# Layer 0 attention written out by unit: V product one tile behind, squares of three units on GpSimd, no factors for a fifth unit

## The chip, the cores and the metric

The kernel runs on one core of one Trainium2 chip. The metric is device time in microseconds (us) of one execution, as the median of several runs. The engines are named as in the profile: PE is TensorE (its weight loads are listed apart as PEld), DVE is VectorE, ACT is ScalarE, POOL is GpSimd, and SP is the engine that here only issues DMAs.

## The reference, cut to what matters

A two-layer decoder trunk on one sequence of 1024 tokens with 1024 channels, in float32. Layer 0 mixes differential attention (4 heads, two softmax maps of 64 channels for each head, 128 value channels) with a pooling mixer, layer 1 a short convolution with dilated attention. Each layer ends in an output projection and a SwiGLU feed-forward block. The change touches layer 0 attention alone:

```python
def diff_attention(q, k, v, lam, slopes):
    def block(i):                       # 128 queries at a time
        s = einsum('bqmhd,bkmhd->bmhqk', qb, k) * scale
        s = s - slopes * dist           # ALiBi
        s = where(dist >= 0, s, -inf)   # causal
        p = softmax(s, axis=-1)
        a = p[:, 0] - lam * p[:, 1]
        return einsum('bhqk,bkhd->bqhd', a, v)
ya = rmsnorm(diff_attention(...), subln_gain) * (1.0 - lambda_init)   # per head, over its 128 channels
x = x + concatenate([ya, yb]) @ w_out
```

The RMS norm of each head is where the squares come from: every output row of 128 values is squared and summed.

## The kernel before

The program is one hand-written stream of instructions for each engine, tied together by counting semaphores. No scheduler orders anything: an engine runs its instructions in the order written, and each `wait_ge` in front of one holds back all that stands behind it on that engine.

Layer 0 attention runs over four **units** u, one for each head, and in each over eight **tiles** i of 128 queries. The causal rule makes tile i as wide as its 128(i+1) keys. The two softmax maps are m = 0 and m = 1. One step i does this:

- `score(m, i+2)` on PE (L682, L683) writes the scores of map m, two tiles ahead, into PSUM. It waits until DVE has read the tile before from the same PSUM place.
- `biased(m, i+1)` on DVE (L1610) adds bias and mask, writes to `PR[m][(i+1)%2]` and takes the row maximum. For map 0 it waits until `turn(i-1)` has read the buffer that it overwrites.
- `expo(m, i+1)` on ACT (L1157) takes the exponentials and their row sum.
- `combine(i)` on DVE (L1635, L1636, L1639) forms map 0 minus lambda times map 1, in place in `PR[0]`. L1639 has two inputs in SBUF.
- `turn(i)` on PE (L700) transposes the i+1 blocks of that tile into PSUM, `turned(i)` on ACT (L1005, to `PT`) copies them to SBUF, and `weigh(i)` on PE (L716) multiplies them by V.
- `scaled(i)` on ACT divides by the row sums. It reads the product twice: L1184 squares it into a junk tile `YJ` with the sum of squares in `YSS`, then L1005 writes `Y`.

PE's order in a step is score 0, turn(i), score 1, weigh(i). Only at i = 6 is turn(6) put ahead of score 0, because that score belongs to the next unit and waits for more.

The scores are made of split factors: each float32 operand is held as a high part in fp32r and the remainder. The high and low parts of a unit's K are stacked in `K1`, of its Q in `QST`, and `K2` is `K1` with its halves exchanged. For the **next** unit, ACT writes the high parts (`next_stack`: two of K at i = 1 and 2, four of Q at i = 6), POOL subtracts to get the low parts (L603), and as soon as the two K parts are complete, SP exchanges the halves with four DMAs (L470, L471). PE waits for these DMAs (`staged`) before tile 0 of the next unit, which is `score(0, 8)` of this unit, issued at i = 6. In unit 3 all of this is also done for a unit 4 that does not exist; two tiles of its scores are computed too.

POOL then adds epsilon to the unit's eight sums of squares (L609) and raises them to -0.5 (L611), and goes on to the K parts of the unit after. The pairs of units run in a loop of two passes over two written units.

Once attention is over, ACT copies four channels' blocks and the first output weights, DVE splits them, and PE goes on with the output projection.

## Time and profile before

| what | value |
| --- | --- |
| median of 3 runs | 2380.04 us (2377.31 to 2386.82) |
| the profiled execution, its own time | 2379.5 us |
| its span, first to last instruction | 2377.7 us |
| mean granted PE clock over the span | 0.982 |
| busy share of the span | PE 95%, DVE 55%, ACT 34%, POOL 20% |

The page cuts the span in 40 equal slices of 59 us. In almost all of them PE is busy nine tenths or more. Layer 0 attention is the dip in slices 4 to 6 (from about 224 to 355 us), where PE falls to seven tenths while DVE and ACT rise to eight tenths. Layer 1 attention is a like dip around 1500 us and is not touched. The times in the rows are us from the span's start.

### The profile page before, as it was taken

The numbers are of one execution on the slowest core, as the hardware profiler recorded it, in microseconds if no ns is written. First come the engines' busy times: TensorE is split into PE (matmuls) and PEld (weight loads), VectorE is DVE, ScalarE is ACT, GpSimd is POOL, SyncE is SP. The second block draws the span as 40 slices with busy tenths as digits, with TensorE's granted clock in tenths as the row PEclk, the third lists the DMA queues.
The fourth block names the chain that finished last, engine by engine and source line by source line (L and its number), as shares of the span: only waits on it lengthen the run. The fifth ranks groups of instructions, "written<-read, shape, count | busy, mean of one in ns | idle before, by whom it ended". The sixth has DMA issues, their size and how long they took to land.

```text
span 2377.7 us, 30768 instructions
## 1 busy us (share of the span) xinstructions
PE 2267.6 (95%) x10680; PEld 1878.8 (79%) x10680; DVE 1298.9 (55%) x1996; ACT 796.8 (34%) x1367; POOL 486.8 (20%) x358
## 2 busy tenths in 40 slices
PE   7999779999999999999999998989999999999998
PEld 6876667878888888887788877888878888888886
DVE  4335767755555555555412236666755555555554
ACT  4124882432222222222311126661532222222221
POOL 0022340332222222221200032220422222222220
PEclk9998999999999999999999998999999999999999
DMA  4021112011111111112111111111021111111112
GB/s 171 13 72 36 36 35 71 18 45 54 53 53 53 53 53 53 53 54 71 36 29 60 37 61 36 36 36 53 18 58 54 53 53 52 51 52 52 52 51 93
DMA packets 138271, 123.14 MB, mean 52 GB/s; under 512 B 6096, under 2 KB 113104, under 8 KB 138192
## 3 DMA queue, kind: packets, MB, share of 16 engines
q1 hardware_dynamic: 137904, 122.05, 16.9%
q8 instruction: 48, 0.79, 0.1%
q14 instruction: 31, 0.25, 0.0%
q10 hardware_dynamic: 288, 0.05, 0.0%
HBM read 107.40 MB, written 4.19 MB: 47 GB/s over the span
## 4 chain that ended last, share of the span: by engine, by line
PE 71%; issue 20%; ACT 4%; DVE 3%; POOL 2%; DMA 0%; DVEq 0%; POOLq 0%; ACTq 0%; SPq 0%
PE PS L964 11%; PE PS L965 11%; PE PS L966 11%; PE PS L630 9%; PE PS L632 9%; PE PS L631 9%; PE PS L716 4%; PE PS L700 2%; POOL QRS L593 1%; ACT PR L1157 1%; PE PS L682 1%; PE PS L683 1%; PE PS L648 1%; ACT PT L1005 1%; PE PS L919 0%
## 5 line engine op out<-in xcount | busy, mean ns | idle before, releaser
L1393 DVE TENSOR_TENSOR SLOTl<-SLOT,RING 128x512 fp32r<-128x512 f32 x294 | 203.4, 694 | 153.4 <-ACT RING L1005 153.4
L557 POOL TENSOR_TENSOR SLOT<-SLOT,SLOT 128x512 f32<-128x512 f32 x168 | 231.9, 1380 | 146.2 <-PE PS L966 103.0
L630 PE MATMUL PS<-WDh,HIDh 128*128 128x512 f32 x640 | 249.0, 389 | 0.0
L631 PE MATMUL PS<-WDl,HIDh 128*128 128x512 f32 x640 | 249.0, 389 | 0.0
L632 PE MATMUL PS<-WDh,HIDl 128*128 128x512 f32 x640 | 249.0, 389 | 0.0
L1819 DVE TENSOR_TENSOR X<-PS,X 128x512 f32<-128x512 f32 x320 | 212.1, 680 | 33.3 <-PE PS L632 33.2
L564 POOL TENSOR_TENSOR P<-U,P 128x512 f32<-128x512 f32 x42 | 54.3, 1293 | 802.6 <-DVE U L1788 802.6
L1005 ACT ACTIVATE RING<-SLOT 128x512 fp32r<-128x512 f32 x294 | 175.4, 623 | 105.3 <-POOL SLOT L557 67.5
L716 PE MATMUL PS<-V,PT 128*128 x864 | 117.7, 283 | 27.2 <-ACT PT L1005 23.5
L964 PE MATMUL PS<-B1h,RING 128*128 128x512 f32 x336 | 132.7, 395 | 8.8 <-DVE SLOTl L1393 8.8
L716 PEld LDWEIGHTS PS<-V,PT 128*128 128x128 f32 x864 | 107.3, 196 | 42.3 <-ACT PT L1005 28.1
L631 PEld LDWEIGHTS PS<-WDl,HIDh 128*128 128x128 f32 x640 | 120.1, 188 | 24.9
L630 PEld LDWEIGHTS PS<-WDh,HIDh 128*128 128x128 f32 x640 | 120.1, 188 | 24.9
L632 PEld LDWEIGHTS PS<-WDh,HIDl 128*128 128x128 f32 x640 | 120.1, 188 | 24.9
L1795 DVE TENSOR_TENSOR HID<-PS,U 128x512 f32<-128x512 f32 x42 | 29.1, 692 | 201.8 <-PE PS L966 201.8
L965 PE MATMUL PS<-B1l,RING 128*128 128x512 f32 x336 | 132.3, 394 | 0.0
L966 PE MATMUL PS<-B1h,SLOTl 128*128 128x512 f32 x336 | 132.3, 394 | 0.0
L593 POOL TENSOR_TENSOR QRS<-QMS,EXPO 128x8 f32<-128x8 f32 x32 | 52.0, 1637 | 390.4 <-DVE QMS L1544 390.2
L630 PE MATMUL PS<-WOh,HH 128*128 128x512 f32 x256 | 103.3, 404 | 10.8 <-DVE WOl L1393 10.0
L1610 DVE CUSTOM_DVE_ANT_0 PR<-PS,BIAS 128x128 f32<-128x128 f32 (+7 forms) x132 | 97.4, 740 | 29.7 <-PE PS L700 20.1
L1470 DVE TENSOR_TENSOR X<-PS,X 128x512 f32<-128x512 f32 x128 | 84.9, 686 | 49.0 <-PE PS L632 48.7
L1157 ACT ACTIVATE PR<-PR,NMX 128x128 f32<-128x128 f32 (+7 forms) x132 | 100.2, 760 | 14.6 <-DVE NMX L1610 13.9
(277 smaller groups left out, 5321.1 us busy)
## 6 DMA issues: line engine op xcount, KB each, us to landing
SLOT<-in_ffn_w_gate SPq DMA_DIRECT2D x84, 256.0 KB, 3.0
SLOT<-in_ffn_w_up SPq DMA_DIRECT2D x84, 256.0 KB, 2.8
WDs<-in_ffn_w_down SPq DMA_DIRECT2D x40, 512.0 KB, 3.5
K<-K SPq DMA_DIRECT2D x32, 256.0 KB, 4.4
RG<-in_od_w_in SPq DMA_DIRECT2D x12, 512.0 KB, 3.8
RQ<-in_ev_w_in SPq DMA_DIRECT2D x8, 512.0 KB, 3.8
RD<-in_ev_w_out SPq DMA_DIRECT2D x4, 1024.0 KB, 4.9
RQ<-in_od_w_in SPq DMA_DIRECT2D x8, 512.0 KB, 3.7
```

The source lines that it names most:

```text
L557: nc.gpsimd.tensor_tensor(at_w[dst], at_w[x], at_w[y], op).then_inc(w_sum, 1)
L630: pe.matmul(dst, lh, rh, start=first, stop=False)
L631: pe.matmul(dst, lh, rl, start=False, stop=False)
L632: return pe.matmul(dst, ll, rh, start=False, stop=last)
L716: last = pe.matmul(weighed(L, m, i), PT[m][:, P * j:P * j + P], V[:, j, bass.ds(off, w)], start=(j == 0), stop=(j == i))
L964: pe.matmul(dst, lh, rh[:, k, :], start=k == 0 and not adds_on, stop=False, skip_group_check=adds_on)
L965: pe.matmul(dst, lh, rl[:, k, :], start=False, stop=False, skip_group_check=adds_on)
L966: last = pe.matmul(dst, ll, rh[:, k, :], start=False, stop=k == 3, skip_group_check=adds_on)
L1005: return nc.scalar.activation(dst, src, ACT.Copy, **kw)
L1157: nc.scalar.activation(pr, pr, ACT.Exp, bias=NMX[:, c:c + 1], scale=-1.0, accum_out=DEN[:, c:c + 1]).then_inc(s_ex[m][L], 1)
L1393: return v.tensor_tensor(dst, src, hi.bitcast(F32), ALU.subtract)
L1819: v.tensor_tensor(xs, bank(4 + t % 4), xs, ALU.add).then_inc(fd_add[L], 1)
```

## The change

The two-pass loop of layer 0 becomes four units written out, with constant semaphore counts and addresses. Within that:

- **PE.** The order of a step becomes score 0, weigh(i-1), turn(i), score 1. The special order at i = 6 is gone, and its waits on `staged` and the low parts now stand in front of score 0, weigh(5) and turn(6). `PT` has two buffers (the second was idle in this layer), `RDN` four columns of pairs.
- **ACT.** `scaled` runs two tiles behind. The squares (L1184) are kept for unit 3 alone. The last step of unit 3 has no exponentials for a next unit.
- **POOL.** For units 0, 1 and 2 the squares come here, as eight instructions for each half unit: one product of 128x512, six additions that fold 128 columns to 2, and one that gives the sum. They stand behind the low parts of the next unit and ahead of the low parts of the unit after.
- **Fifth unit.** No high or low parts, no DMAs, no bias table and no scores for it.
- Layer 1 keeps its loop; its counts are adapted.

```diff
+                def squares(u, half):
+                    n = 8 * (2 * u + half)
+                    pool.wait_ge(o_ok[0][0], 2 + NT * u + 4 * half + 4)
+                    ys = Y[:, 4 * half:4 * half + 4, P * u:P * u + P]
+                    nc.gpsimd.tensor_tensor(YQ[:], ys, ys, ALU.mult).then_inc(y_fold, 1)
+                    for k, w in enumerate((64, 32, 16, 8, 4, 2)):
+                        pool.wait_ge(y_fold, n + k + 1)
+                        nc.gpsimd.tensor_tensor(YQ[:, :, 0:w], YQ[:, :, 0:w], YQ[:, :, w:2 * w], ALU.add).then_inc(y_fold, 1)
+                    ...
+                if L == 0:
+                    pool.wait_ge(mx_pe, 4)
+                    for u in range(UNITS):
+                        if u + 1 < UNITS:
+                            for k in range(STACKS):
+                                low_stack(k, (u + 1) % 2, u + 1, stacks_before(0, u + 1) + k)
+                            pool.wait_ge(stack_lo, stacks_before(0, u + 2))
+                            squares(u, 0)
+                            squares(u, 1)
+                        else:
+                            pool.wait_ge(y_sq, NT)
...
-                            if L == 0:
-                                if i == NT - 2:
-                                    turn(L, 0, g, h, i)
-                                    pe.wait_ge(staged[1 - b], 64 * (3 * L + it + 2) if b else 64 * (2 * L + it + 1))
-                                    pe.wait_ge(stack_lo, following + 3)
-                                    score(L, 0, b, g, i + 2)
-                                    pe.wait_ge(stack_lo, following + 4)
-                                else:
-                                    score(L, 0, b, g, i + 2)
-                                    turn(L, 0, g, h, i)
-                                score(L, 1, b, g, i + 2)
-                                weigh(L, 0, u, g, h, i)
+                            if i == NT - 2 and more:
+                                pe.wait_ge(staged[1 - b], 64 * (u // 2 + b + 1))
+                                pe.wait_ge(stack_lo, following + 3)
+                            if more:
+                                score(0, 0, b, g, i + 2)
+
+                            if i > 0:
+                                weigh(0, 0, u, g, 0, i - 1)
+                            elif u > 0:
+                                weigh(0, 0, u - 1, g - NT, 0, NT - 1)
+                            turn(0, 0, g, 0, i)
+                            if i == NT - 2 and more:
+                                pe.wait_ge(stack_lo, following + 4)
+                            if more:
+                                score(0, 1, b, g, i + 2)
...
+                            if i == NT - 2 and not last:
+                                next_stack(g, 1 - b, u + 1, 2, 3)
+                            if i < NT - 1 or not last:
+                                expo(0, g, i + 1)
+                            if g + i >= 2:
+                                scaled(g + i - 2)
+                            if i < NT - 1 or not last:
+                                expo(1, g, i + 1)
+                            turned(0, g, i)
+                            if i in (1, 2) and not last:
+                                next_stack(g, 1 - b, u + 1, i - 1)
+                            if i == NT - 2 and not last:
+                                next_stack(g, 1 - b, u + 1, 4, 5)
```

PE at i = 6 of unit 0, before. `K_166` and `QST_75` are the next unit's factors; the rows with IDN and PR are turn, those with V and PT weigh.

```order
L700 MATMUL PS<-IDN,PR_176 128x128 [waits c_ok]
L700 MATMUL PS<-IDN,PR_176 128x128 x6
L823 ISA
L824 REGISTER_ALU [waits staged1]
L676 REGISTER_ALU [waits stack_lo]
L682 MATMUL PS<-K_166,QST_75 128x128 [waits s_mxA0]
L683 MATMUL PS<-K_170,QST_75 128x128
L826 REGISTER_ALU
L682 MATMUL PS<-K_167,QST_76 128x128 [waits s_mxB0,stack_lo]
```

The same place now:

```order
L708 MATMUL PS<-K_166,QST_75 128x128 [waits s_mxA0,stack_lo,staged1]
L709 MATMUL PS<-K_170,QST_75 128x128
L744 MATMUL PS<-V,PT_175 128x128 [waits o_okA0,t_eaA0]
L744 MATMUL PS<-V,PT_175 128x128 x5
L728 MATMUL PS<-IDN,PR_176 128x128 [waits c_ok,t_eaA0]
L728 MATMUL PS<-IDN,PR_176 128x128 x6
L708 MATMUL PS<-K_167,QST_76 128x128 [waits s_mxB0,stack_lo]
L709 MATMUL PS<-K_171,QST_76 128x128
```

The wait for the DMAs (staged1) moved from behind turn(6) to ahead of it, and weigh(5) stands between the two.

POOL between the last low part of a unit and the first of the unit after, before:

```order
L603 TENSOR_TENSOR QST_76<-QK,QST_76 64x768
L607 ISA
L609 ISA [waits stack_lo,y_sq]
L609 TENSOR_TENSOR YSS<-YSS,EPSP 128x8
L611 REGISTER_ALU [waits y_ms]
L611 TENSOR_TENSOR YRS<-YSS,EXPO 128x8
L601 ISA [waits y_rs]
L602 REGISTER_ALU [waits stack_hi]
L603 TENSOR_TENSOR K_164<-QK,K_164 64x1024 [waits stack_lo]
```

And now; the eight rows from `YQ<-Y` to `YSS<-YQ` stand there twice, the second half unit's are left out here:

```order
L602 TENSOR_TENSOR QST_76<-QK,QST_76 64x768 [waits stack_lo,stack_hi]
L609 TENSOR_TENSOR YQ<-Y 128x512 [waits o_okA0,stack_lo]
L612 TENSOR_TENSOR YQ<-YQ 128x4x64 [waits y_fold]
L612 TENSOR_TENSOR YQ<-YQ 128x4x32 [waits y_fold]
L612 TENSOR_TENSOR YQ<-YQ 128x4x16 [waits y_fold]
L612 TENSOR_TENSOR YQ<-YQ 128x4x8 [waits y_fold]
L612 TENSOR_TENSOR YQ<-YQ 128x4x4 [waits y_fold]
L612 TENSOR_TENSOR YQ<-YQ 128x4x2 [waits y_fold]
L615 TENSOR_TENSOR YSS<-YQ 128x4 [waits y_fold]
...
L630 TENSOR_TENSOR YSS<-YSS,EPSP 128x8 [waits y_fold]
L632 TENSOR_TENSOR YRS<-YSS,EXPO 128x8 [waits y_ms]
L602 TENSOR_TENSOR K_166<-QK,K_166 64x1024 [waits stack_lo,stack_hi,y_rs]
```

Sixteen instructions, each waiting for the one before, came between the low parts of one unit and the K parts of the unit after.

## Rows read from the trace of the kernel before

**Rows 1.** Windows: us, PE, PEld, DVE, ACT, POOL busy; clock, DMA share, GB/s.

```profile
224.00:370.00 146.00, 110.39 (x658) 91.03 (x659) 104.00 (x248) 114.21 (x289) 50.42 (x32) 0.92 0.14 37
```

**Rows 2.** Waits from 224 to 375 us: us in total, times, longest.

```profile
PE PS L716 <- ACT PT L1005: 23.5, 29, 1.6
...
DVE PR L1610 <- PE PS L700: 20.1, 15, 3.5
```

**Rows 3.** Timeline of PE, unit 1, i = 3 to 6: start, us, form.

```profile
271.04 0.60 PE L700 MATMUL PS<-IDN,PR 128*128 128x128 f32 x4
...
275.30 0.71 PE L700 MATMUL PS<-IDN,PR 128*128 128x128 f32 x5
...
277.06 1.38 PE L716 MATMUL PS<-V,PT 128*128 x10 [0.22 <-ACT PT L1005]
278.19 0.48 PE L682 MATMUL PS<-K,QST 128*128 128x512 f32 x1
...
279.20 0.82 PE L700 MATMUL PS<-IDN,PR 128*128 128x128 f32 x6
...
281.66 1.60 PE L716 MATMUL PS<-V,PT 128*128 x12 [0.68 <-ACT PT L1005]
...
283.80 0.30 PE L682 MATMUL PS<-K,QST 128*128 128x128 f32 x1
```

**Rows 4.** Timeline of DVE, units 1 and 2.

```profile
276.20 1.09 DVE L1610 CUSTOM_DVE_ANT_0 PR<-PS,BIAS 128x896 f32<-128x896 f32 x1 [0.88 <-PE PS L700]
...
277.72 1.02 DVE L1639 SCALAR_TENSOR_TENSOR PR<-PR,SCB,PR 128x768 f32<-128x768 f32 x1
...
293.65 1.28 DVE L1579 SCALAR_TENSOR_TENSOR BIAS<-DIST,SM,MASK 128x1024 f32<-128x1024 f32 x1
```

**Rows 5.** Timeline of ACT, unit 1.

```profile
278.56 0.37 ACT L1184 ACTIVATE YJ<-PS,RDN 128x128 f32<-128x128 f32 x1
...
285.33 0.90 ACT L1005 ACTIVATE PT<-PS 128x896 f32<-128x896 f32 x1
```

**Rows 6.** Timeline of POOL, end of unit 1 and start of unit 2.

```profile
287.04 3.90 POOL L603 TENSOR_TENSOR QST<-QK,QST 64x768 fp32r<-64x768 f32 x2 [2.56 <-ACT QST L1005]
293.15 0.20 POOL L609 TENSOR_TENSOR YSS<-YSS,EPSP 128x8 f32 x1 [2.21 <-ACT YJ L1184]
293.53 1.64 POOL L611 TENSOR_TENSOR YRS<-YSS,EXPO 128x8 f32 x1 [0.17 <-POOL YSS L609]
298.54 2.37 POOL L603 TENSOR_TENSOR K<-QK,K 64x1024 fp32r<-64x1024 f32 x1 [3.38 <-ACT K L1005]
301.92 2.37 POOL L603 TENSOR_TENSOR K<-QK,K 64x1024 fp32r<-64x1024 f32 x1 [1.00 <-ACT K L1005]
```

**Rows 7.** The last of four exchange DMAs of unit 2, and landing of L471.

```profile
306.11 1.12 SPq L471 DMA_DIRECT2D K<-K  x1
...
DMA to landing us min/median/max: 2.3/3.8/5.6
```

**Rows 8.** Timelines of POOL and DVE where both read SBUF.

```profile
458.38 1.29 POOL L541 TENSOR_TENSOR F0T3s<-F0T2s,F0T3s 128x512 f32<-128x512 f32 x1
...
248.71 0.72 POOL L603 TENSOR_TENSOR QST<-QK,QST 64x256 fp32r<-64x256 f32 x1 [8.66 <-ACT QST L1005]
249.67 1.30 POOL L603 TENSOR_TENSOR QST<-QK,QST 64x256 fp32r<-64x256 f32 x1 [0.23 <-POOL QST L603]
...
248.88 1.49 DVE L1639 SCALAR_TENSOR_TENSOR PR<-PR,SCB,PR 128x896 f32<-128x896 f32 x1
```

**Rows 9.** Timeline of PE: score(0, 8) of units 0 and 2.

```profile
251.17 0.31 PE L682 MATMUL PS<-K,QST 128*128 128x128 f32 x1
...
314.94 0.30 PE L682 MATMUL PS<-K,QST 128*128 128x128 f32 x1
```

**Rows 10.** Windows, columns as in rows 1: PE nearly idle, then its clock.

```profile
252.00:254.00 2.00, 0.42 (x4) 0.35 (x4) 1.16 (x5) 2.00 (x4) 0.00 (x0) 1.00 0.00 0
...
256.00:258.00 2.00, 2.00 (x12) 2.00 (x11) 0.00 (x0) 1.10 (x5) 1.76 (x2) 0.51 0.00 0
```

More of the change, by code:

```diff
@@ L808, in _ @@
                         score(L, m, 0, 0, i)
-                with pe.Fori(0, 2) as it:
-                    for b in range(2):
-                        u = 2 * it + b
-                        g, h = 16 * it + 8 * b, 8 * it + 4 * b
-                        following = stacks_before(L, u + 1)
+                if L == 0:
+                    for u in range(UNITS):
+                        b, g = u % 2, NT * u
+                        following = stacks_before(0, u + 1)
                         for i in range(NT):
+                            more = u + 1 < UNITS or i < NT - 2
@@ new lines, in _ @@
+                            turn(0, 0, g, 0, i)
[3 more added lines that the diff above has]
+                                score(0, 1, b, g, i + 2)
+                    weigh(0, 0, UNITS - 1, NT * (UNITS - 1), 0, NT - 1)
+                else:
+                    with pe.Fori(0, 2) as it:
+                        for b in range(2):
+                            u = 2 * it + b
+                            g, h = 16 * it + 8 * b, 8 * it + 4 * b
+                            following = stacks_before(L, u + 1)
+                            for i in range(NT):
+                                if i == 0:
+                                    pe.wait_ge(stack_lo, following)
+                                if i == 2 and b == 0:
+                                    pe.wait_ge(staged_rest, 64 * L + 64)
@@ new lines, in scaled @@
+                def scaled(n):
+                    u, i = n // NT, n % NT
+                    c = 2 * (i % 4)
+                    act.wait_ge(o_pe[0][0], n + 1)
+                    if u == UNITS - 1:
+                        act.wait_ge(o_ok[0][0], n + 2)
+                        nc.scalar.activation(YJ[:], weighed(0, 0, i), ACT.Square, scale=RDN[:, c:c + 1],
+                                             accum_out=YSS[:, n:n + 1]).then_inc(y_sq, 1)
+                    copy(Y[:, i, P * u:P * u + P], weighed(0, 0, i), scale=RDN[:, c:c + 1]).then_inc(o_ok[0][0], 1)
@@ new lines, in _, with turned, scaled, next_bias @@
+                if L == 0:
+                    for u in range(UNITS):
+                        b, g, last = u % 2, NT * u, u + 1 == UNITS
+                        for i in range(NT):
+                            if i < NT - 1 or not last:
+                                biased(0, b, g, i + 1)
+                            if i == 1 and not last:
+                                dve.wait_ge(s_mx[1][0], g + 1)
+                                bias(0, 1 - b, u + 1)
+                            combine(g, i)
+                            if i < NT - 1 or not last:
+                                biased(1, b, g, i + 1)
+                else:
+                    with dve.Fori(0, 2) as it:
+                        att.reg = per_iter * it
+                        for b in range(2):
+                            u = 2 * it + b
+                            g = 16 * it + 8 * b
+                            def turned(m, i):
+                                if i >= 4:
+                                    dve.wait_ge(t_pe[m][L], g + i + 3)
+                                    w = P * (i + 1)
+                                    v.tensor_copy(PT[m][:, HALF:w], turn_bank(1, m, i, 1)[:, 0:w - HALF]).then_inc(t_ed[m][1], 1)
+                            def scaled(m, i):
+                                c = m + 2 * (i % 2)
+                                dve.wait_ge(s_ex[m][1], g + i + 1)
+                                att.link(v.reciprocal(RDN[:, c:c + 1], DEN[:, c:c + 1]))
+                                dve.wait_ge(o_pe[m][1], g + i + 1)
+                                v.tensor_scalar(Y[:, i, bass.ds(u * P + HD * m, HD)], weighed(1, m, i), RDN[:, c:c + 1], None,
+                                                ALU.mult).then_inc(o_ok[m][1], 1)
+                            def next_bias(m):
+                                dve.wait_ge(s_mx[m][1], g + 9)
+                                bias(m, 1 - b, 2 * u + 2 + m)
+                            for i in range(NT):
```

227 lines of the change are left out of this document (99 added, 128 removed).

## The prediction

> **What bounds the kernel now.** First the windows over the attention stage of layer 0 [rows 1]: of 146 us ACT is busy 114, PE 110, DVE 104, POOL 50. No engine is full, so the stage runs at the pace of a chain that crosses engines, and the question for each edit is whether it stands on that chain. Next the list of waits [rows 2]: PE waits 23.5 us in 29 places for ACT's copy of the transposed tile, and DVE 20.1 us for the transposes. So the chain is turn, copy, product with V, next score, next turn. The timeline of PE shows one round of it [rows 3]: turn(4) starts at 275.30, weigh(4) at 277.06 behind the copy, score(0, 7) at 278.19, turn(5) at 279.20. That is 3.90 us a step, and PE is in order, so the product and the score both stand between two turns.
>
> **V product one tile behind.** The step becomes score 0, weigh(i-1), turn(i). This looks as if it took the product out of the chain, but the score put ahead of it has a wait of its own. score(0, 7) needs biased(0, 6), and biased(0, 6) overwrites the buffer that turn(4) reads. It starts at 276.20, 0.19 after turn(4) ends [rows 3, 4]. The new round from turn(4) to turn(5) is therefore turn 0.71, handover 0.19, biased 1.09, handover 0.06, score 1.01 (278.19 to 279.20), weigh 1.13 (277.06 to 278.19): 4.19 us, 0.3 more than now [rows 3, 4]. One tile earlier each piece is smaller (0.11, 0.13, 0.12 and 0.23), 3.6 in all, against 4.26 measured from 271.04 to 275.30: 0.6 less [rows 3]. The product's cost grows fastest with i, so the order gains at small i. I take two steps at 0.6, one small one at 0.1, minus 0.3: **1.0 us a unit**, between 0 and 2. In units 1 and 2 it counts only if nothing later holds the unit back, and something does.
>
> **Squares off ACT.** 24 squares leave ACT, 0.36 us each from start to start (278.56 to 278.92), 8.6 us in all [rows 5]. The rounds above do not pass through them. They are slack on ACT, and I count nothing for them in units 0 to 2; the bound from the other side is a rival below.
>
> **Squares on POOL.** For each half unit, the 128x512 product costs 1.29 [rows 8]. 64x256 takes 0.72 and 64x768 half of 3.90 less a gap, 1.83, so 0.54 us for each 256 columns above a fixed 0.18 [rows 6, 8]. The folds have 256, 128, 64, 32, 16, 8 and 4 elements: 0.72, 0.45, 0.31, 0.25, 0.21, 0.20 and 0.19. With the product that is 3.6 us. Each waits for the one before; that gap is 0.17 between the two statistics instructions and 0.23 between two low parts [rows 6, 8]. Eight gaps make 1.4 to 1.9. A half is 5.0 to 5.5, I take 5.1, **10.2 us a unit**. POOL was two thirds idle, so by busy time this is free. By place it is not: it stands ahead of the K parts that the next score(0, 8) waits for.
>
> **The chain that this makes**, from one score(0, 8) to the next:
> - On PE score 0.3, weigh(5) 1.4, turn(6) 0.95, then a handover 0.1 to ACT: 2.8. The shift of the wait ahead of turn(6) puts this piece on the chain.
> - From ACT's copy of tile 6 to the end of the last low part: 285.33 to 290.94, 5.6 [rows 5, 6].
> - Squares 10.2.
> - Epsilon and power, from 293.15 to 295.17 and a handover: 2.2 [rows 6].
> - Two K parts: 2.37 each and a gap, 4.9 [rows 6].
> - The DMAs: the K parts end at 304.29, the last of four is issued at 306.11 and lands 3.8 later (median): 5.6 [rows 6, 7].
>
> The sum is 31.3 us. It can't run undisturbed. DVE's two-input instructions and POOL shut each other out: L1639 with 896 columns took 1.49 at 248.88 while POOL worked from 248.71 to 249.43, and the POOL instruction behind took 1.30 instead of 0.72 [rows 8]. In the 17 us of squares, power and K parts, DVE has six combines of 128 to 768 columns. The widest takes 1.02 and each narrower one 0.13 less (1.28 at 1024 columns), 4.2 in all, and the bias table 1.28 [rows 4]. Seven gaps of 0.2 take up 1.4, which leaves 4.1. The Trainium skill, SBUF — State Buffer, section "Who interferes with whom", says that whichever starts first holds the shared ports for its whole instruction. By that rule the whole of each counts, as I do; if the two ran side by side, the forecast would be 8.2 us lower. **35.4 us a unit.**
>
> Measured now from score(0, 8) of unit 0 to that of unit 2: 63.8 us for two units [rows 9]. Two rounds of 35.4 are 70.8: **plus 7.0**. PE would run out of work at i = 6 of units 1 and 2 for some 5 us each.
>
> **The clock.** When PE was busy 0.42 of 2 us, its granted clock was 0.51 two windows later, which is the 1.2 GHz level [rows 10]. After a stall, the 2.7 us of PE work at the head of the chain would take twice as long. This counts once inside the two rounds and may count again after unit 2: **plus 2.7**, between 0 and 5.4.
>
> **What is gained at the ends.** Before score(0, 8) of unit 0: 1.0. After that of unit 2: unit 3 gains 1.0 by the order, 1.1 by the bias table of a fifth unit (1.28 on DVE right ahead of combine(1), [rows 4]), 0.6 because tiles 6 and 7 are no longer mixed with factors on ACT, and 0.7 in the last two steps of unit 2. Sum 3.4. The squares stay there, and so does the tail (last turn, copy, product, scaling). The earlier place of score(0, 8) inside step 6 shifts both ends by the same amount and cancels. **Minus 4.4**, between 2 and 7. Constant counts instead of registers I count at nothing: the waits in question are attributed to other engines [rows 2, 4].
>
> **Sum.** 7.0 + 2.7 - 4.4 = +5.3 us on the profiled execution's own 2379.5 us: **2384.8 us**. That execution lies 0.5 under the median of 2380.04, so against the median the change is +0.2%. About 0.5%, 12 us, is what a measurement of this kernel can tell from no change.
>
> **Rivals.**
> 1. *The POOL chain is short enough.* Gaps of 0.17, the locked ports cost little, the clock stays: 31.3 x 2 - 63.8 = -1.2, minus 4.4: 2373.9. For it: POOL often fits between two combines today. Against it: with POOL never idle, each combine must meet it. Chance 0.17.
> 2. *ACT sets the pace.* It is the busiest engine [rows 1]. Then 8.6 us of squares and the fifth unit's six high parts go (0.9 and 1.7 at tiles 6 and 7, two K parts of 1.0, as the factors of other units cost), some 13 us: 2366. For it: the profile's chain names ACT often. Against it: it needs POOL's round under 28 us, less than its own rows sum to. Chance 0.13.
> 3. *Slower: the small folds are dear.* There are 16 short instructions in a round, 32 in two. The median run leaves the 0.5% band when the two rounds cost 6.6 more, that is from 0.21 us more for each. At 0.3 more it is +9.6: 2394.4. For it: the power of eight elements takes 1.64 [rows 6], so a short instruction is not always a cheap one, and a form of four rows of 2 to 64 columns is nowhere in the trace. Against it: the addition of 128x8 takes 0.20 [rows 6]. A second fall of the clock adds to it. Chance 0.20.
> 4. My forecast, a round of 34 to 37 us: 0.50, all of it within 12 us of now.
>
> **Range and chances.** The low end takes in rival 1 and a bit of rival 2's gain, the high end rival 3 with 0.3 us: 2371 to 2396. Faster by over 0.5%: 0.13. Within: 0.66. Slower: 0.21.
>
> **What would show it.** In the profile after: in units 1 and 2 PE idles several us ahead of the first score of the next unit, released by the DMA K<-K; from one such score to the next 34 to 37 us, where it was 31.1 and 32.6; POOL busy without a break from the last low part to the second K part, at 10 to 11 us for the squares; in unit 0 no such wait, and turn(4) to turn(5) about 4.2. Unit 3 two to three us shorter than before; the granted clock at 0.5 behind the stalls. Wrong if the first score of the next unit never waits for a DMA (then rival 2 or a round shorter than I think), or if YQ instructions of few elements take 0.4 and more (rival 3).

## The result and the profile after

The changed kernel takes 2388.52 us (median of 20 runs, 2381.31 to 2393.81), the kernel before on the same chip 2379.55 (median of 20, 2376.99 to 2386.82). The ratio is 1.0034, with an interval of 1.0025 to 1.0043. That is inside the 0.5% that the prediction took as the limit of no change, but it is a real loss: 8 us by the ratio, 9 by the medians. The profiled execution took 2390.1 us with a span of 2388.1, which is 10.4 us more than the span before.

Where do these 10.4 us come in? Both profiles start layer 0 attention, turn(0) of unit 0, at 227.33 us, so marks can be compared directly:

| mark | before | after | difference |
| --- | --- | --- | --- |
| turn(6) of unit 0 | 250.43 | 251.25 | +0.8 |
| turn(6) of unit 2 | 314.24 | 320.13 | +5.9 |
| turn(6) of unit 3 | 345.23 | 348.98 | +3.8 |
| first product of the output projection | 361.66 | 367.66 | +6.0 |
| first power of the norm behind it | 422.78 | 427.63 | +4.9 |
| first `biased` of layer 1 attention | 1440.99 | 1447.38 | +6.4 |
| last `biased` of layer 1 attention | 1587.74 | 1600.24 | +12.5 |
| end | 2377.7 | 2388.1 | +10.4 |

So 6 us come from the attention stage that was changed, and as much again from layer 1 attention, whose text is the same; 2 us come back behind it. These are single executions, and the marks move between executions of one text. But two of the runs below have the same instructions in this stage, the one that moves layer 1's loop (as changed) and the one that adds transposes alone (as before), and they give nearly the same difference: from turn(0) of unit 0 to the first output product 137.9 and 131.5 us, 6.3 apart, where here it is 140.3 and 134.3.

The first group of windows (us, busy us of PE, PEld, DVE, ACT, POOL; granted clock, DMA share, GB/s) shows the stage that [rows 1] showed of before:

```profile
224.00:370.00 146.00, 110.38 (x630) 91.65 (x631) 102.07 (x236) 101.83 (x231) 64.14 (x74) 0.87 0.10 25
```

ACT has lost 12 us of work and POOL has gained 14, as planned, but PE's granted clock has gone from 0.92 to 0.87. The list of waits from 224 to 375 us, against [rows 2]:

```profile
PE PS L708 <- POOL QST L602: 10.1, 6, 1.8
ACT PT L1047 <- PE PS L728: 10.0, 7, 3.3
```

The 23.5 us of PE behind ACT's copies are nearly gone (5.3 are left); that is the V product moved one tile back. A wait that was short before has come in: PE's score for the low part of Q that POOL writes. PE's timeline has it twice in a unit, at i = 6 (128 columns) and at i = 0 (384 columns):

```profile
249.62 0.30 PE L708 MATMUL PS<-K,QST 128*128 128x128 f32 x1 [1.59 <-POOL QST L602]
...
284.06 0.30 PE L708 MATMUL PS<-K,QST 128*128 128x128 f32 x1 [1.56 <-POOL QST L602]
...
285.70 0.93 PE L728 MATMUL PS<-IDN,PR 128*128 128x128 f32 x7
...
292.88 0.44 PE L708 MATMUL PS<-K,QST 128*128 128x384 f32 x1 [1.76 <-POOL QST L602]
...
318.49 0.30 PE L708 MATMUL PS<-K,QST 128*128 128x128 f32 x1 [1.58 <-POOL QST L602]
```

These are the rows that answer to [rows 9]. From 249.62 to 284.06 and from there to 318.49 it is 34.4 us each. Behind the first wait of a unit stand weigh(5) and turn(6), behind the second weigh(7) and turn(0). Not all of them could have run in the gap. At i = 6 ACT's copy for weigh(5) ends at 282.86 and DVE's combine for turn(6) only at 284.90, after the wait is over:

```profile
282.07 0.79 ACT L1047 ACTIVATE PT<-PS 128x768 f32<-128x768 f32 x1
283.40 1.50 DVE L1686 SCALAR_TENSOR_TENSOR PR<-PR,SCB,PR 128x896 f32<-128x896 f32 x1
```

At i = 0 the copy for weigh(7) ends at 291.94, 0.9 before the score.

POOL's timeline of the same unit, against [rows 6]:

```profile
254.49 3.91 POOL L602 TENSOR_TENSOR QST<-QK,QST 64x768 fp32r<-64x768 f32 x2 [3.44 <-ACT QST L1047]
258.48 1.04 POOL L609 TENSOR_TENSOR YQ<-Y 128x512 f32<-128x512 f32 x1
259.60 3.43 POOL L612 TENSOR_TENSOR YQ<-YQ 128x256 f32<-128x256 f32 x6
263.11 0.20 POOL L615 TENSOR_TENSOR YSS<-YQ 128x4 f32<-128x4 f32 x1
263.38 1.04 POOL L609 TENSOR_TENSOR YQ<-Y 128x512 f32<-128x512 f32 x1
264.50 3.00 POOL L612 TENSOR_TENSOR YQ<-YQ 128x256 f32<-128x256 f32 x6
267.57 0.20 POOL L615 TENSOR_TENSOR YSS<-YQ 128x4 f32<-128x4 f32 x1
267.85 0.20 POOL L630 TENSOR_TENSOR YSS<-YSS,EPSP 128x8 f32<-128x8 f32 x1
268.14 1.64 POOL L632 TENSOR_TENSOR YRS<-YSS,EXPO 128x8 f32<-128x8 f32 x1
269.86 5.14 POOL L602 TENSOR_TENSOR K<-QK,K 64x1024 fp32r<-64x1024 f32 x2
283.24 2.25 POOL L602 TENSOR_TENSOR QST<-QK,QST 64x256 fp32r<-64x256 f32 x2 [8.24 <-ACT QST L1047]
```

The squares take 9.3 us a unit (258.48 to 267.77), and the K parts are done at 275.0. Then POOL is idle for 8.24 us. The last exchange DMA is issued behind them (SP's queue, against [rows 7]):

```profile
277.10 0.78 SPq L473 DMA_DIRECT2D K<-K  x1
```

Its issue ends at 277.88. With the median landing time of [rows 7], 3.8, that makes 281.7, and with the longest of this line in the stage, 5.1, 283.0. The score goes at 284.06, so the K chain is not what ends last. DVE, on the other side of the shared port, against [rows 4]:

```profile
263.38 1.32 DVE L1686 SCALAR_TENSOR_TENSOR PR<-PR,SCB,PR 128x256 f32<-128x256 f32 x1
...
266.81 0.62 DVE L1686 SCALAR_TENSOR_TENSOR PR<-PR,SCB,PR 128x384 f32<-128x384 f32 x1
...
271.03 1.74 DVE L1686 SCALAR_TENSOR_TENSOR PR<-PR,SCB,PR 128x512 f32<-128x512 f32 x1
```

The combine of 256 columns takes twice as long as that of 384. And PE's clock in these windows:

```profile
262.00:264.00 2.00, 0.71 (x4) 0.44 (x3) 1.93 (x4) 0.71 (x3) 1.84 (x3) 1.00 0.00 0
264.00:266.00 2.00, 1.15 (x4) 0.79 (x4) 1.49 (x4) 0.79 (x3) 1.76 (x4) 0.69 0.00 0
266.00:268.00 2.00, 2.00 (x7) 1.36 (x6) 1.93 (x7) 2.00 (x5) 1.61 (x6) 0.50 0.00 0
268.00:270.00 2.00, 2.00 (x9) 1.90 (x10) 0.27 (x3) 1.26 (x4) 1.84 (x3) 0.50 0.00 0
```

PE was busy 0.71 and 1.15 of 2 us there, and then it runs at 0.50, the 1.2 GHz level. The same fall comes again at 298 to 305 us. The kernel before has no fall in the middle of unit 1 or 2; its fall of [rows 10] lies ahead of turn(0) of unit 1.

The tail of unit 3, on PE. Before, turn(7) took 1.03 and weigh(7) 2.05:

```profile
348.98 0.95 PE L728 MATMUL PS<-IDN,PR 128*128 128x128 f32 x7 [0.16 <-DVE PR L1686]
352.10 2.10 PE L744 MATMUL PS<-V,PT 128*128 128x128 f32 x14 [2.17 <-ACT PT L1047]
354.00 1.92 PE L728 MATMUL PS<-IDN,PR 128*128 128x128 f32 x8
357.02 3.62 PE L744 MATMUL PS<-V,PT 128*128 128x128 f32 x16 [1.11 <-ACT PT L1047]
```

Last, DVE in layer 1 attention, at the first `biased` of the second pass of the loop, before and after:

```profile
1518.60 0.42 DVE L1610 CUSTOM_DVE_ANT_0 PR<-PS,BIAS 128x256 f32<-128x256 f32 x1 [0.40 <-issue]
```

```profile
1529.24 0.42 DVE L1668 CUSTOM_DVE_ANT_0 PR<-PS,BIAS 128x256 f32<-128x256 f32 x1 [3.13 <-issue]
```

DVE stands for 3.13 us although nothing in the profile holds it back, and PE waits 4.00 us for it where it waited 1.27.

### The profile page after: what moved, and what is told of

Its sections match the earlier page's. It is cut to its first block, busy times and chain, and to the rows that moved or that the text cites. A ratio compares the mean times of both kernels' runs of the same rounds, so it can differ in the third digit from the quotient of the medians.

```text
span 2388.1 us, 30402 instructions
## 1 busy us (share of the span) xinstructions
PE 2276.0 (95%) x10672; PEld 1886.9 (79%) x10672; DVE 1301.8 (55%) x1991; ACT 784.9 (33%) x1309; POOL 500.5 (21%) x400
## 3 DMA queue, kind: packets, MB, share of 16 engines
HBM read 107.40 MB, written 4.19 MB: 47 GB/s over the span
## 4 chain that ended last, share of the span: by engine, by line
PE 67%; issue 14%; DVE 2%; POOL 1%; ACT 1%; DVEq 0%; POOLq 0%; ACTq 0%
PE PS L1006 11%; PE PS L1007 11%; PE PS L1008 11%; PE PS L656 9%; PE PS L658 9%; PE PS L657 9%; PE PS L744 2%; PE PS L728 1%; POOL QRS L595 1%; PE PS L708 1%; PE PS L674 1%; PE PS L709 0%; PE PS L961 0%; PE PS L960 0%; PE PS L959 0%
## 5 line engine op out<-in xcount | busy, mean ns | idle before, releaser
L1880 DVE TENSOR_TENSOR X<-PS,X 128x512 f32<-128x512 f32 x320 | 212.5, 681 | 33.3 <-PE PS L658 33.2
L744 PE MATMUL PS<-V,PT 128*128 (+1 forms) x864 | 118.3, 284 | 7.5 <-ACT PT L1047 5.3
L708 PE MATMUL PS<-K,QST 128*128 128x512 f32 (+2 forms) x196 | 85.6, 437 | 32.6 <-DVE NMX L1668 15.5
```

The source lines that it names most:

```text
L708: pe.matmul(dst, q, K1[b][m][:, c0:c1], start=True, stop=False)
L744: last = pe.matmul(weighed(L, m, i), PT[m if L else i % 2][:, P * j:P * j + P], V[:, j, bass.ds(off, w)], start=(j == 0), stop=(j == i))
L1880: v.tensor_tensor(xs, bank(4 + t % 4), xs, ALU.add).then_inc(fd_add[L], 1)
```

## The experiments

The experiments ran on three occasions, four kernels each. Absolute times are compared only within one; over all of them the ratio to the kernel before counts, and the lengths inside the profiles. "A unit" is the distance of two turn(6) from each other, unit 0 to 1 and unit 1 to 2. It is 34.5 and 34.4 us in the changed kernel, and 32.7 and 31.1 before. The 32.7 holds the fall of the clock of [rows 10]: in the run with the transposes alone, which has the same instructions there and no fall, it is 31.0 and 31.1.

### Squares back on ACT

```diff
-                            squares(u, 0)
-                            squares(u, 1)
-                        else:
-                            pool.wait_ge(y_sq, NT)
+                        pool.wait_ge(y_sq, NT * u + NT)
...
-                    if u == UNITS - 1:
+                    if True:
                         act.wait_ge(o_ok[0][0], n + 2)
```

> The changed kernel with the squares of all four units back on ScalarE (all else as changed). Marks are the first score of the next unit, score(0, 8), in units 0, 1 and 2, and the first product of the output projection; in the changed kernel 249.6, 284.1, 318.5 and 367.7 us, so 34.4 us from mark to mark. Theory A (the squares on GpSimd keep VectorE's combine off the shared ports in steps 0 to 2 of each unit, 1.0 + 1.3 + 1.1 us): 31.0 us from mark to mark, and combines of 0.35, 0.48 and 0.75 us again, for 1.1, 1.3 and 1.7. Theory B (ScalarE was the relief that mattered, 0.36 us for each square): the gain by the ports is eaten by 8 x 0.36 us on ScalarE, and it stays at 33 to 34.5 us. Theory C, my prediction (a chain through GpSimd and the DMAs): also about 31, with the DMAs no longer last. The whole: A -6 to -7 us against the changed kernel, so about +2 us against the kernel before; B no change.

Measured: 2385.66 us, ratio 1.0022 (1.0012 to 1.0031). A unit takes 32.1 and 32.4. So the squares on POOL cost 2.2 us a unit in this order of PE. The combine of 256 columns is back at its own length:

```profile
261.16 0.48 DVE L1685 SCALAR_TENSOR_TENSOR PR<-PR,SCB,PR 128x256 f32<-128x256 f32 x1
...
267.01 0.75 DVE L1685 SCALAR_TENSOR_TENSOR PR<-PR,SCB,PR 128x512 f32<-128x512 f32 x1
```

1.32 - 0.48 and 1.74 - 0.75 make 1.8 us a unit that DVE lost to POOL. The kernel is still slower than before, so the squares are not the whole of it.

### No squares at all in units 0 to 2

```diff
-                            squares(u, 0)
-                            squares(u, 1)
+                            pool.wait_ge(o_ok[0][0], 2 + NT * u + NT)
```

> The changed kernel without any squares in units 0 to 2, on no engine (their sums of squares are a constant 1.0). Theory A: 31.0 us from mark to mark, the same as with squares on ScalarE, since ScalarE has slack. Theory B: clearly less than with the squares on ScalarE, by up to 2.9 us a unit.

Measured, one execution: 2384.66 us; a unit takes 32.1 and 32.3, the same as with the squares on ACT. ACT has room for them: they cost nothing there, so taking them away could gain nothing. That settles rival 2.

### PE's two waits behind the work that doesn't need them

```diff
+                            if early:                      # i in (0, NT - 2)
+                                behind()                   # weigh of the tile before
+                            if i == NT - 2 and early:
+                                turn(0, 0, g, 0, i)
                             if i == 0:
                                 pe.wait_ge(stack_lo, following)
                             if i == NT - 2 and more:
                                 pe.wait_ge(staged[1 - b], 64 * (u // 2 + b + 1))
                                 pe.wait_ge(stack_lo, following + 3)
                             if more:
                                 score(0, 0, b, g, i + 2)
...
```

In the other steps weigh and turn stay behind the score.

> The changed kernel, but in step 6 TensorE does the V product and the transposes of tile 6 ahead of the wait for the next unit's factors, and in step 0 the V product of the last tile ahead of the wait for the last low parts. Squares stay on GpSimd. Theory A: the two waits of 1.6 and 1.8 us in front of the scores cost nothing any more, 2.2 us less from mark to mark counted at tile 6's transposes (32.2 instead of 34.4). Theory C: the chain from mark to mark loses TensorE's piece of 2.8 us, so 31.6 or whatever else binds. Rival: they cost nothing as it is, because VectorE's combines set the pace there: 34.4.

> The changed kernel with PE's two waits behind the work that doesn't need them, squares on POOL as in the changed kernel: the same text as the run with one look, now timed against the kernel before. If the two waits are what the new order costs: 2375 again, 4 us under the kernel before, ratio about 0.998. If that look was luck of one execution: 2380 or more.

Measured: one execution gave 2375.35 us. Timed on the next occasion, the same text took 2379.06 (ten runs, 2377.77 to 2382.54), ratio 1.0001 (0.9992 to 1.0011). The first was a good execution, not a typical one: in its profile the granted clock fell less often in layer 1 attention. What holds in both profiles is the unit, 31.5 us in the first and 31.5 and 31.3 in the second. So with both waits moved a unit is 3.0 us shorter, and with the squares on POOL and this order the loss against before is gone.

The 1.6 and 1.8 us of the waits sum to 3.4, which looks like the same amount, but they are not what comes back. From turn(5) to turn(7) it is 9.1 us with the wait at i = 6 in front and 9.1 with it behind. From turn(7) to turn(0), where the other wait stands, 5.27 become 4.39. The rest, 2.1 us, comes from the steps between turn(0) and turn(4). DVE's combines meet POOL there still:

```profile
262.42 1.13 DVE L1694 SCALAR_TENSOR_TENSOR PR<-PR,SCB,PR 128x384 f32<-128x384 f32 x1
...
269.08 1.96 DVE L1694 SCALAR_TENSOR_TENSOR PR<-PR,SCB,PR 128x640 f32<-128x640 f32 x1
```

Without POOL they take 0.62 and 0.89, so DVE loses 1.6 us a unit, nearly as much as in the changed kernel. What is mostly missing is the fall of the clock. With PE's new order and the wait at i = 0 in front, units 1 and 2 had one in their first steps 9 times out of 10, over five profiles; with both waits behind, 2 times out of 12, over six. But the fall alone isn't the price either: the unit of 31.3 us has one.

### The order of the kernel before, with the rest of the change

Squares on ACT, four units written out, no factors for a fifth unit, but weigh(i) in its own step and turn(6) ahead of the waits:

```diff
+                            if i == NT - 2:
+                                turn(0, 0, g, 0, i)
...
                             if more:
                                 score(0, 1, b, g, i + 2)
-                    weigh(0, 0, UNITS - 1, NT * (UNITS - 1), 0, NT - 1)
+                            weigh(0, 0, u, g, 0, i)
```

> TensorE's order of the kernel before (the V product in its own tile's step, tile 6 transposed ahead of the waits), squares of all units on ScalarE, written out by unit and without the factors, table and scores of a fifth unit. What is left of the change is then the written-out form, ScalarE's scaling two tiles behind, two buffers for the transposed tile, and no fifth unit. Theory A: 31.1 us from unit to unit as before, unit 3 shorter by 1 to 2 us, but its tail, where TensorE now has little to do, may fall to the lower clock level as in the changed kernel (last transposes 1.92 us instead of 1.03) and cost 2 us: first product of the output projection at 360 to 362 us (before 361.7). The whole: -2 to +1 us against the kernel before. Rival (the order with the product one tile behind is itself a gain, 0.6 us in two steps of each unit): this one is slower than the run with squares on ScalarE.

Measured: 2381.69 us, ratio 1.0008 (0.9998 to 1.0018). A unit takes 31.0 and 31.0, and the first output product comes 130.2 us after turn(0) of unit 0, where it was 134.3 before. The attention stage is thus 4.1 us shorter in the profile and the kernel no faster. Most of the 4.1 is the execution that it is compared with: the run with the transposes alone has the old stage with fewer falls of the clock and takes 131.5, so the stage gains about 1.3. Layer 1 takes that away: DVE stands 2.95 us at the loop's second pass here too, as in every kernel of this study in which DVE's layer 0 is written out and nothing else moves the loop.

### Both: squares on ACT and the waits behind

> The changed kernel with both edits at once: the squares of all units on ACT, and PE's two waits for the next unit's factors behind the work that doesn't need them (weigh(7) at i = 0; weigh(5) and turn(6) at i = 6). Theory A (squares on POOL lengthen DVE's combines through the shared port, and with the waits in front this is passed on; with the waits behind, part of it is absorbed): a unit 30.9 to 31.3 us against 31.5 with the squares on POOL, the first output product 1 to 2 us earlier than there, time 2373 to 2375. Theory D (with the waits behind, the place of the squares no longer matters): 31.5 a unit, 2375. Theory B (ACT is relieved by the change and needs it): a unit 32 or more, 2378 or more.

> The text with squares on ACT and both waits behind, timed a second time. It took 2384.4, though in its profile the attention stage is 0.5 us shorter than with the squares on POOL, which took 2379.1; and the same text with the transposes of the identity took 2376.0. If 2384.4 holds: something outside layer 0 attention differs between two texts that differ in 24 instructions. If it comes out at 2378 to 2380: an earlier level of this text on that occasion, and differences of some 4 us between runs of one occasion are then no evidence.

Measured: 2384.36, ratio 1.0025 (1.0015 to 1.0034), and on the next occasion 2382.33, ratio 1.0010 (1.0001 to 1.0019). Inside the first of the two profiles a unit takes 30.9 and 30.9, the shortest of all. Theory A's numbers for the unit hold: with the waits behind, the squares on POOL cost 0.5 us a unit, no longer 2.2. And the product with V one tile behind is worth nothing: 30.9 here, 31.0 in its own step.

Step by step, from turn(6) of unit 1 to turn(6) of unit 2:

| step, us | before | changed | squares on ACT | waits behind | both |
| --- | --- | --- | --- | --- | --- |
| turn(6) to turn(7) | 5.08 | 4.15 | 4.15 | 4.79 | 4.79 |
| turn(7) to turn(0) | 4.39 | 5.27 | 5.28 | 4.39 | 4.59 |
| turn(0) to turn(4) | 13.86 | 15.87 | 13.84 | 13.76 | 13.01 |
| turn(4) to turn(5) | 3.90 | 4.19 | 4.20 | 4.22 | 4.22 |
| turn(5) to turn(6) | 3.90 | 4.95 | 4.95 | 4.31 | 4.32 |

Either edit alone takes 2 us out of turn(0) to turn(4), and both together 2.9, so the 2.2 and the 3.0 don't add up. How large the loss there is depends on which combines meet POOL and on whether the clock is down at the time; the runs don't split it further.

But the whole time fits none of the theories. It lies 2 to 6 us above the text with the squares on POOL, though its units are shorter, and where those microseconds lie differs from one execution to the next: in the profile of the second occasion the clock fell twice more, at the start of unit 1 and behind its turn(6). Why this text should draw more such falls than its neighbour is open.

### Filling PE's idle stretches at the end of the stage

```diff
+                            if u == UNITS - 1 and i >= NT - 2:
+                                pe.wait_ge(s_mx[0][0], g + 9)
+                                warm(12 if i == NT - 2 else 6)
                     weigh(0, 0, UNITS - 1, NT * (UNITS - 1), 0, NT - 1)
+                    warm(32)
```

> As the run with squares on ACT and waits behind, plus transposes of the identity on PE into a PSUM place that nobody reads: 12 after turn(6) of unit 3, 6 after turn(7), 32 after weigh(7), at 0.13 us each by turn(7). They do no work; they fill PE's idle stretches at the end of the stage. Theory T (the tail of unit 3 and the start of the output projection are slow because PE ran idle there and its granted clock fell to 0.50; the two tiles of scores of the fifth unit had filled that gap before): turn(7) takes 1.03 and weigh(7) 2.05 again, the tail from turn(6) to the first output product 16.5 us instead of 18.7, and the products after it run at a granted clock near 1.00, another 2 us: 3 to 4 us less than the run without them. Against it: if the clock falls all the same, or the tail waits for ACT and DVE, the time is the same within 1 us, or more by the transposes themselves.

Measured: 2375.97 us, ratio 0.9989 (0.9979 to 0.9999), 8.4 us under the same text without them on the same chip. PE's timeline of the tail:

```profile
341.85 1.83 PE L745 MATMUL PS<-V,PT 128*128 128x128 f32 x14 [0.86 <-ACT PT L1060]
...
345.66 2.05 PE L745 MATMUL PS<-V,PT 128*128 128x128 f32 x16 [0.46 <-ACT PT L1060]
347.55 3.66 PE L711 MATMUL PS<-IDN 128*128 128x128 f32 x32
354.74 0.47 PE L653 MATMUL PS<-WOh,HH 128*128 128x512 f32 x1 [3.54 <-DVE WOl L1466]
355.05 0.40 PE L654 MATMUL PS<-WOl,HH 128*128 128x512 f32 x1
...
356.29 0.63 PE L655 MATMUL PS<-WOh,HL 128*128 128x512 f32 x1
```

The same text without them had a fall of the clock in weigh(6):

```profile
344.05 3.36 PE L741 MATMUL PS<-V,PT 128*128 128x128 f32 x14 [2.17 <-ACT PT L1052]
```

With them weigh(6) takes 1.83, turn(7) 1.04 instead of 1.17, and turn(6) to the first output product 16.0 us (338.72 to 354.74) instead of 17.6; the 18.7 of the changed kernel is the longest of all. After the 32 transposes PE idles 3.54 us, and the clock still falls a few products later (0.63 for a product instead of 0.40). The tail and the products behind it, up to the first power of the norm, explain 2.8 of the 8.4 us. In the two profiles layer 1 attention differs by another 6.0 (156.26 and 150.25), with more falls of the clock in the longer one; why, stays open.

The idle 2.17 us are there in all ten profiles without a fifth unit and without transposes. The clock fell behind them in nine. In one, the first with the waits behind, it didn't, and its tail takes 16.0 us without any filling. So the fall is likely there, not certain.

### Layer 1's loop at another place in the program

```diff
                         split_qk(L, r)
+                        if L == 1 and r in (2, 3):
+                            for _ in range(96):
+                                dve.sem_inc(waited, 1)
```

> The changed kernel with 192 semaphore increments more on DVE, 96 each behind two splits of layer 1's weights where DVE waits 10 to 15 us anyway. They move all later DVE instructions by 192 places. Theory F (the 3.13 us that DVE stands without a releaser between the two passes of layer 1's attention loop, 0.40 in the kernel before, is the fetch of instructions behind a taken branch, and depends on where in the program the loop lies): the 3.13 changes, to about 0.4 if the new place is a good one, and PE's wait there from 4.0 to 1.3. Theory G (it comes from the data or the queues of the new layer 0): it stays at 3.1. Place a little further or nearer may be needed: one look can show F but not exclude it.

Measured, one execution: 2384.64 us. DVE at the second pass of the loop, and PE's score that waits for it:

```profile
1521.87 0.42 DVE L1671 CUSTOM_DVE_ANT_0 PR<-PS,BIAS 128x256 f32<-128x256 f32 x1 [0.42 <-issue]
```

```profile
1522.36 0.44 PE L708 MATMUL PS<-K,QST 128*128 128x384 f32 x1 [1.29 <-DVE NMX L1671]
```

The 3.13 us have become 0.42 and PE's wait is 1.29 again, with nothing changed but the number of instructions ahead of the loop. So the stall belongs to the place of the loop in DVE's program, and not to the new layer 0. The Trainium skill, Runtime: NRT & Kernel Launch, section "Instruction fetch mechanics", says that an engine prefetches instructions in order, in two blocks, and that a taken branch to a target outside them waits for a fetch; this fits what the runs show, and the runs add the price, 2.7 us. Distance from the first to the last `biased` of layer 1 attention: 146.75 us before, 152.86 after, 148.76 here.

### All of it

The two waits behind, squares on ACT, the transposes (54 instead of 32 at the end), the 192 increments:

> The changed kernel with everything that the runs so far point to: squares on ACT, PE's two waits behind, the transposes of the identity at the end of the stage (54 instead of 32 after weigh(7), so that they reach up to the first output product), and the 192 semaphore increments on DVE that move layer 1's loop. If the three effects are separate and add up: 2376.0 (the run without the last two edits) minus 2.7 for the loop of layer 1 minus about 0.8 for the first twelve output products at 0.40 us apart from 0.63: 2372 to 2373.5, ratio 0.9975. If layer 1's stall is made up by what follows it, as a rival says: 2375 to 2376.

Measured: 2372.95 us (6 runs), against 2380.22 of before on the same chip; ratio 0.9964 (0.9951 to 0.9976). This beats both kernels, that of before by 7 us in the medians and 8.6 by the ratio. The sum came out as expected, but not each term on its own, against the profile with 32 transposes: layer 1 attention is 1.5 us shorter (148.80 against 150.25 us) and not 2.7, since the clock fell at 1476 to 1482 us where it hadn't there; the stretch ahead of it is 1.2 us longer; and the output projection gains 1.6 us instead of 0.8. A unit takes 30.9, turn(6) of unit 3 to the first output product 16.1, and the products there start at full clock:

```profile
349.90 6.06 PE L711 MATMUL PS<-IDN 128*128 128x128 f32 x54
357.13 0.47 PE L653 MATMUL PS<-WOh,HH 128*128 128x512 f32 x1 [1.17 <-DVE WOl L1466]
357.43 0.39 PE L654 MATMUL PS<-WOl,HH 128*128 128x512 f32 x1
357.66 0.40 PE L655 MATMUL PS<-WOh,HL 128*128 128x512 f32 x1
357.89 0.40 PE L653 MATMUL PS<-WOh,HH 128*128 128x512 f32 x1
```

### The transposes alone, in the kernel before

```diff
+                if L == 0:
+                    pe.wait_ge(s_mx[0][0], 8 * UNITS + 2)
+                    for _ in range(54):
+                        pe.transpose(PS[:, 0:P], IDN[:], IDN[:])
```

> The kernel before, with 54 transposes of the identity on PE after the last weigh(7) of layer 0 and nothing else. Theory T (the clock at the start of the output projection costs time in both kernels): the first 12 output products 0.23 us apart instead of 0.43, 2.4 us in all, so 2376.5, ratio 0.999. If what follows is set by DVE's splits and not by PE: no change.

Measured: 2376.75 us, ratio 0.9987 (0.9978 to 0.9996), as theory T has it. In its profile the output projection up to the first power of the norm takes 58.6 us, where it was 61.1. About a third of what the best version gains can be had without the change.

### Only the wait at i = 6 behind

> The changed kernel with only one of PE's two waits moved: at i = 6 weigh(5) and turn(6) stand ahead of the waits and of the first score of the next unit; at i = 0 the wait for the four low parts of Q stays ahead of weigh(7) and turn(0). Squares on POOL. With both moved a unit took 31.5 us, with none 34.4. If each wait is paid for by its own length (1.6 at i = 6, 1.8 at i = 0): 33.0 to 33.3 a unit. If the wait at i = 0 alone spoils it: 34 or more. If it is only the one at i = 6: 31.5.

Measured, one execution: 2387.5 us, and the two units differ: 33.7 and 31.2. They are the same instructions. In the first, the clock fell at 264 to 270 us and one combine met POOL for long; in the second it didn't:

```profile
272.40 2.81 DVE L1694 SCALAR_TENSOR_TENSOR PR<-PR,SCB,PR 128x640 f32<-128x640 f32 x1
...
305.30 0.98 DVE L1694 SCALAR_TENSOR_TENSOR PR<-PR,SCB,PR 128x640 f32<-128x640 f32 x1
```

The second unit is as short as with both waits moved, though the wait at i = 0 stands ahead of weigh(7) and turn(7) to turn(0) takes 5.29 us: turn(0) to turn(4) takes only 12.65 there, and 15.07 in the first. So none of the three expectations fits both units. The waits have no fixed price; a fall of the clock, and the collisions that shift with it, make 2.4 us in one unit, more than either wait's own cost.

## Why the prediction was right, and where it was not

The forecast was 2384.8 us, 0.2% more, from a sum of +5.3 us; measured is +0.34%, 8 to 9 us. The range holds it and the side is right. But the steps did not all do what they were said to do, and errors cancelled: that the sum came near was luck. Every term of the sum lies ahead of the first output product, where the two profiles differ by +6.0; the rest of the 8 to 9 us was in no term. Measured from turn(6) to turn(6):

| piece | forecast | measured |
| --- | --- | --- |
| up to turn(6) of unit 0 | -1.0 | +0.8 |
| units 1 and 2, clock included | +9.7 | +5.1 |
| from there to the first output product | -3.4 | +0.1 |
| layer 1 attention | 0 | +6.1, of it 2.7 by the loop's place |

- **V product one tile behind.** The hand-worked rounds were right to the tenth: turn(4) to turn(5) is 4.19 in unit 3 of the changed kernel (340.85 to 345.04), and turn(3) to turn(4) 3.61. But the 1.0 us a unit is not there: 30.9 with the new order, 31.0 with the old one, squares on ACT in both. Between these two, turn(2) to turn(4) gains 0.7 (7.17 against 7.90), where the sum had 1.3 for three steps, and not only turn(4) to turn(5) loses 0.4 but turn(5) to turn(6) too. The sum charged one late step and left out the second.
- **Squares off ACT.** Nothing, as said; the run without any squares shows it.
- **Squares on POOL.** 9.3 us instead of 10.2. The product of an operand with itself takes 1.04, where the bound row with two operands had 1.29 [rows 8]; the folds of 64 elements and fewer cost 0.20 to 0.33 each where nothing meets them (0.56 and 1.06 for the one of 8 elements when it met DVE), so rival 3 falls.
- **POOL's chain to the K DMAs.** This is the step that failed. Its undisturbed sum was good: up to the landing of the last DMA the round takes 34.4 less 2.4, 32.0, against 31.3. But the 4.1 us for the shared port were put on POOL, which lost 0.7 (1.6 if the squares' shorter length is counted). It was DVE that lost, 1.8 a unit, on the chain of combine and turn. The rule of the Trainium skill (SBUF — State Buffer, "Who interferes with whom") is that the engine that issues first holds the shared ports and the other waits. DVE's 1.74 for 512 columns and 1.32 for 256 agree with it, and so does the other way round: POOL's fold of 8 elements took 1.06 instead of 0.20 when DVE's bias table had started 0.34 ahead of it. Which engine is the later one must come from rows, and here it was mostly DVE.
- **What PE waits for.** The prediction named the DMA K<-K as the releaser of the first score of the next unit, and it never is. By the prediction's own sign ("Wrong if the first score of the next unit never waits for a DMA") the mechanism was wrong, and the round of 34.4 inside its 34 to 37 was luck. It is the low part of Q, a few steps away: last score of the unit, ACT's high part, POOL's low part. That chain stood in the kernel before as well (POOL's low parts at 281.99 and 287.04, the second in [rows 6]), but there turn(6) and the products with V lay ahead of the waits, and PE waited 0.3 us for them in unit 1. The prediction put turn(6) and weigh(5) behind the wait on POOL's chain and missed the second wait, at i = 0, that now holds back weigh(7). Against the 31.1 of before a unit is 3.3 us longer: 0.9 at i = 0, 2.0 between turn(0) and turn(4), 0.3 at turn(4) to turn(5) by the order, and 0.1 around i = 6, where the prediction had some 5 us.
- **The clock.** Forecast 2.7, once, behind a stall. There were two falls in the middle, in the first steps of units 1 and 2 (from 264 and 298 us), and a third that was not forecast, in the tail (from 352 us), ahead of the one at the start of the output projection that the kernel before has too (from 356 us there). Also, the 63.8 us of [rows 9] that the two rounds were compared with hold a fall themselves, that of [rows 10]; without it, in the run with the transposes alone, two units take 62.1.
- **The ends.** Unit 3 from turn(0) to turn(6) is 2.1 us shorter (19.4 after, 21.5 before), where the sum had 2.7. The 1.0 of it for the order is not there: with the old order and no fifth unit it is 19.5. And "the tail stays" was wrong: turn(6) to the first output product takes 18.7 instead of 16.4, and 17.4 to 17.7 in the other profiles with a fall there. The scores of a fifth unit were work without use, and they kept PE busy where it now idles 2.17 us and then mostly runs at half its clock. No rival of the prediction had this.
- **Layer 1.** Nobody's term. Writing four units out makes DVE's program longer ahead of layer 1's loop and moves it to a place where the jump back costs 2.7 us more. The other 3.4 us of +6.1 go with falls of the clock at i = 1 and 2 of a unit, which come in some executions and not in others: one text has 150.3 and 156.2 us in its two profiles (waits behind, squares on POOL). The fall in the second unit came in 10 of 12 profiles of written-out kernels and in neither of the two with the old loop; two are too few to say that the change makes it likelier.

Of the signs named beforehand, those of PE's idle place (right place, wrong releaser, and 1.6 us instead of several), of 34 to 37 us a round, of unit 3 and of turn(4) to turn(5) came true; POOL without a break did too (254.49 to 275.0), but it then stood idle for 8 us. "In unit 0 no such wait" did not: the wait of 1.59 us is there at 249.62.

## What to carry to other kernels

When a wait moves in an engine's queue, look at what now stands behind it and when each piece of it was ready: here one wait of 1.6 us cost nothing by itself and another of 1.8 cost 0.9. Idle PE time can cost more than its length, since here the clock mostly fell behind it; work that looks useless may be what keeps the clock up, so before removing it ask what fills its place. One profile is not enough for this: the falls come and go between executions of one text. And where loops are written out, look at the same loops further on: here a gap without a releaser at the head of a second pass was a matter of place, and could be moved away.

## What the runs showed of the hardware

- At the jump back of layer 1's loop DVE stood 0.40 us in the kernel before and its variant, 0.42 in the two kernels moved by 192 instructions, and 2.90 to 3.20 us in all others. The two texts that were profiled twice showed it both times.
- POOL's addition of 128x4 elements takes 0.20 us and the power of 128x8 1.64; six dependent folds from 256 down to 8 elements a partition take 2.6 us with their gaps where nothing meets them, and up to 3.7 where they met DVE.
- DVE's combine of 128x640 took between 0.88 and 2.89 us by when it met POOL.
- A chain of 128x128 transposes of the identity, 0.11 us each, kept the granted clock at 1.00 at the end of the stage, and delayed nobody where it ended before the next operand was there.
